# Sums of squares in a gated-delta recurrence: one fp32 product, or two single-pass products of a rounded and a remaining part

## The reference

```python
def gdn_mixer(h, w_in, w_conv, a_log, dt_bias, w_onorm, w_out):
    proj = h @ w_in
    ...
    qkv = jax.nn.silu(causal_conv(qkv, w_conv))
    q, k, v = jnp.split(qkv, 3, axis=-1)
    ...
    q = q * lax.rsqrt(jnp.sum(q * q, axis=-1, keepdims=True) + EPS) * (1.0 / math.sqrt(d))
    k = k * lax.rsqrt(jnp.sum(k * k, axis=-1, keepdims=True) + EPS)
    ...
    o = chunk_gated_delta(q, k, v, g, beta)
    o = o * lax.rsqrt(jnp.mean(o * o, axis=-1, keepdims=True) + EPS) * w_onorm.astype(jnp.float32)
    return (o.reshape(B_, S, GDN_WIDTH) * jax.nn.silu(z)) @ w_out
```

## Time and profile before

| | us |
|---|---|
| median of 3 runs | 2057.92 (2056.8 to 2059.51) |
| span of the profiled execution | 2055.0 |
| TensorE busy | 2017.8 (98%) |
| VectorE busy | 1465.0 (71%) |
| ScalarE busy | 569.1 (28%) |
| GpSimd busy | 354.7 (17%) |

### The profile page before, as it was taken

One profiled execution on the slowest core, in us unless ns is written; L12 is line 12 of the kernel. 1 busy time (PEld: TensorE's weight loads), 2 busy tenths in 40 slices (PEclk: granted clock), 3 DMA queues, 4 the chain that ended last, 5 costly groups with the idle time before them and its releaser, 6 DMA issues.

```text
span 2055.0 us, 31779 instructions
## 1 busy us (share of the span) xinstructions
PE 2017.8 (98%) x12910; PEld 1621.5 (79%) x12910; DVE 1465.0 (71%) x2281; ACT 569.1 (28%) x994; POOL 354.7 (17%) x320
## 2 busy tenths in 40 slices
PE   8999999999999999999999999999999999999999
PEld 6888788887777777777778877777888888888887
DVE  5766666667877777667888887566656778949973
ACT  2000122222544444324774234444310010000000
POOL 2212111111101110011111211111112122212221
PEclk9999999999999999999999999999999999999999
DMA  4323222222211121122112332111223332322332
GB/s 161 112 92 103 83 90 86 93 83 75 83 60 57 63 68 61 60 72 82 62 63 73 126 98 88 62 48 45 77 82 103 98 103 92 103 92 93 102 97 88
DMA packets 53361, 173.73 MB, mean 85 GB/s; under 512 B 6336, under 2 KB 6720, under 8 KB 53088
## 3 DMA queue, kind: packets, MB, share of 16 engines
q1 hardware_dynamic: 48112, 161.67, 23.9%
q10 hardware_dynamic: 5104, 10.03, 1.8%
HBM read 169.51 MB, written 2.16 MB: 84 GB/s over the span
## 4 chain that ended last, share of the span: by engine, by line
PE 45%; DVE 6%; ACT 2%; issue 1%; DVEq 0%; ACTq 0%
PE ps_lin L1817 13%; PE ps_lin L1818 13%; PE ps_lin L1819 13%; PE ps_att L1863 4%; PE ps_aux L1863 2%; ACT arena L1271 2%; DVE arena L409 1%; DVE w_lo L409 1%; DVE arena L415 1%; DVE arena L897 1%; PE ps_att L1872 0%; DVE y_lo L409 0%; DVE sq L409 0%; DVE xw_lo L415 0%; DVE x L409 0%
## 5 line engine op out<-in xcount | busy, mean ns | idle before, releaser
L1817 PE MATMUL ps_lin<-xw_hi,w_hi 128*128 128x512 f32 (+1 forms) x1728 | 698.5, 404 | 0.0
L1819 PE MATMUL ps_lin<-xw_hi,w_lo 128*128 128x512 f32 (+1 forms) x1728 | 675.0, 391 | 0.0
L1818 PE MATMUL ps_lin<-xw_lo,w_hi 128*128 128x512 f32 (+1 forms) x1728 | 674.0, 390 | 0.0
L391 POOL TENSOR_SCALAR w_hi<-raw 128x1024 fp32r<-128x1024 f32 (+5 forms) x312 | 349.9, 1122 | 1685.1 <-PE ps_lin L1819 1560.5
L409 DVE TENSOR_TENSOR w_lo<-raw,w_hi 128x1024 fp32r<-128x1024 f32 (+2 forms) x344 | 382.3, 1114 | 48.0 <-POOL w_hi L391 17.6
L1271 ACT ACTIVATE arena<-arena 128x512 f32<-128x512 f32 (+7 forms) x331 | 206.4, 631 | 734.3 <-DVE arena L409 357.6
L1819 PEld LDWEIGHTS ps_lin<-xw_hi,w_lo 128*128 128x128 f32 (+1 forms) x1728 | 322.7, 187 | 71.8
L1817 PEld LDWEIGHTS ps_lin<-xw_hi,w_hi 128*128 128x128 f32 (+1 forms) x1728 | 323.1, 187 | 68.4 <-issue 3.7
L1818 PEld LDWEIGHTS ps_lin<-xw_lo,w_hi 128*128 128x128 f32 (+1 forms) x1728 | 323.4, 187 | 61.1
L409 DVE TENSOR_TENSOR arena<-ps_lin,rstd 128x512 f32<-128x512 f32 (+2 forms) x213 | 146.6, 688 | 201.2 <-PE ps_lin L1819 186.7
L1817 PE MATMUL ps_lin<-y_hi,w_hi 128*128 128x512 f32 (+1 forms) x544 | 205.4, 378 | 1.3 <-DVE w_lo L409 1.1
(11 more groups left out here) (175 smaller groups left out, 1697.2 us busy)
## 6 DMA issues: line engine op xcount, KB each, us to landing
raw<-in_w_up SPq DMA_DIRECT2D x44, 512.0 KB, 3.3
raw<-in_conv_w_in SPq DMA_DIRECT2D x32, 512.0 KB, 3.3
raw<-in_fox_w_in SPq DMA_DIRECT2D x32, 512.0 KB, 3.3
raw<-in_gdn_w_in SPq DMA_DIRECT2D x32, 512.0 KB, 3.2
raw<-in_w_gate SPq DMA_DIRECT2D x24, 512.0 KB, 3.2
raw<-in_swa_w_in SPq DMA_DIRECT2D x20, 512.0 KB, 3.2
raw<-in_w_ml SPq DMA_DIRECT2D x16, 512.0 KB, 3.3
raw<-in_w_down SPq DMA_DIRECT2D x16, 512.0 KB, 3.6
```

Source lines behind the costliest of these rows:

```text
L391: pool.tensor_scalar(w_whole(n, kc * c)[0], w_raw(n, kc * c), 1.0, 0.0, mult, add).then_inc(s("w_rounded"), 1)
L1817: pe.matmul(o, wh, hi, start=first and k == 0, stop=False)
L1818: pe.matmul(o, wh, lo, start=False, stop=False)
L1819: ins = pe.matmul(o, wl, hi, start=False, stop=last and k == kc - 1)
```

## The change

Each square is computed twice on ScalarE: once in fp32 as before, and once rounded to fp32r, into a free part of `y8_hi` (`sq_hi`, two pieces of 256 columns). GpSimd subtracts the rounded from the full square (`sq_lo`), and signals `gdn_sq_low` or `gdn_osq_low`. TensorE multiplies both parts, in fp32r, with fp32r copies of the ones and mean matrices, which VectorE makes at the head of the layer. GpSimd's subtraction is tied to a weight unit: it is issued right behind the rounding of the third unit after the tile (the q or k tile, or the next head's z tile; for the last head behind the unit of the fourth output tile). There is one `sq_hi` and one `sq_lo`, so ScalarE's Squares get waits for the sums that read them. The semaphores of five input DMAs are merged into one.

```diff
--- before.py
+++ after.py
@@ -294,6 +294,10 @@
         A = carve()
         A(2 * XA_H * MEM)
         sq2 = A(3, T)
+        sq_lo = sb("sq_lo", [P, T], f32r)
+        ones_r, mean_r = sb("ones_r", [P, P], f32r), sb("mean_r", [P, P], f32r)
+        sq_hi = y8_hi[:, 1:3, NT * HD:]
+        sq_parts = lambda ap: ap.rearrange("p (a b) -> p a b", a=2)
         rstd_final, mix_w = sb("rstd_final", [P, T]), sb("mix_w", [P, ND])
         swa["sin"] = rstd_final[:]
 
@@ -334,6 +338,11 @@
             src = raw[:, n % RAW, 0:cols]
             return src.rearrange("p (a c) -> p a c", a=2) if n in ASIDE else src
 
+        GDN_LOW = {}
+        for _h in range(GDN_H):
+            GDN_LOW.update({LAST_UNIT[tile_of("gdn_w_in", part * GDN_H + _h)] + SPLIT: ("gdn_sq", 2 * _h + part + 1, 1) for part in range(2)})
+            GDN_LOW[LAST_UNIT[tile_of("gdn_w_in", 3 * GDN_H + _h + 1)] + SPLIT if _h < GDN_H - 1 else LAST_UNIT[tile_of("gdn_w_out", 3)]] = ("gdn_osq", _h + 1, 0)
+
         GDN_FILL = {"tok": 4, "squares": 4, "A": 0, "U0": 3}
         LEVEL_FILL = (0, 2, 2, 1, 1, 2, 1)
         LAST_FILL = sum(GDN_FILL.values())
@@ -361,11 +370,11 @@
                 sp.dma_start(x[:, m, :], a["x"][m]).then_inc(s(X_IN[m][0]), 16)
                 if m in (1, 3):
                     weights((m + 1) // 2)
-            sp.dma_start(mats[:].rearrange("p a b -> p (a b)"), a["mats"]).then_inc(s("mats_in"), 16)
+            sp.dma_start(mats[:].rearrange("p a b -> p (a b)"), a["mats"]).then_inc(s("small_in"), 16)
             sp.dma_start(rows[:], a["rows"]).then_inc(s("small_in"), 16)
             sp.dma_start(freq[:], a["freq"]).then_inc(s("small_in"), 16)
             sp.dma_start(sinks[:], a["sinks"]).then_inc(s("small_in"), 16)
-            sp.dma_start(angle["pos"].bitcast(i32), a["positions"]).then_inc(s("pos_in"), 16)
+            sp.dma_start(angle["pos"].bitcast(i32), a["positions"]).then_inc(s("small_in"), 16)
             for n in range(RAW, len(UNITS)):
                 sp.wait_ge(s("w_split"), n - RAW + 1)
                 weights(n)
@@ -389,6 +398,10 @@
                 elif n >= SPLIT:
                     pool.wait_ge(s("unit_done"), n - SPLIT + 1)
                 pool.tensor_scalar(w_whole(n, kc * c)[0], w_raw(n, kc * c), 1.0, 0.0, mult, add).then_inc(s("w_rounded"), 1)
+                if n in GDN_LOW:
+                    squared, count, at = GDN_LOW[n]
+                    pool.wait_ge(s(squared), count)
+                    pool.tensor_tensor(sq_parts(sq_lo), sq_parts(sq[:, at, :]), sq_hi.bitcast(f32), sub).then_inc(s(squared + "_low"), 1)
 
 
         @block.vector
@@ -521,8 +534,7 @@
             def swa_angles():
 
                 ang, kk, rr = angle["ang"], angle["kk"], swa["sin"]
-                dve.wait_ge(s("pos_in"), 16)
-                dve.wait_ge(s("small_in"), 48)
+                dve.wait_ge(s("small_in"), 80)
                 step(dve.tensor_copy(ang, angle["pos"].bitcast(i32)))
                 step(ts(ang, ang, freq[:], mult))
                 yield
@@ -613,6 +625,8 @@
 
             F = gdn
             R8 = slice(0, 8)
+            dve.tensor_copy(ones_r[:], mat("ones"))
+            dve.tensor_copy(mean_r[:], mat("mean_h")).then_inc(s("mean_set"), 1)
             step(dve.memset(F["u"][:, 0:3], 0.0))
             step(dve.memset(F["ones"][R8, :], 1.0))
             dve.wait_ge(s("rstd_ready"), 3)
@@ -1387,7 +1401,7 @@
 
             F = gdn
             R8 = slice(0, 8)
-            act.wait_ge(s("small_in"), 48)
+            act.wait_ge(s("small_in"), 80)
             step(activation(F["ea"][R8, :], row("gdn_a_log", 8), ACT.Exp))
             act.wait_ge(s("softplus_in"), 2)
             step(activation(F["r3"][R8, :], F["r2"][R8, :], ACT.Abs))
@@ -1426,7 +1440,10 @@
                     act.wait_ge(s("gdn_silu"), 3 * r + part + 1)
                     if 2 * r + part:
                         act.wait_ge(s("gdn_ss"), 2 * r + part)
-                    activation(sq[:, 1, :], dst, ACT.Square).then_inc(s("gdn_sq"), 1)
+                    if part == 0 and r > 1:
+                        act.wait_ge(s("gdn_oss"), r - 1)
+                    activation(sq[:, 1, :], dst, ACT.Square)
+                    activation(sq_hi, sq_parts(dst), ACT.Square).then_inc(s("gdn_sq"), 1)
 
             for part in range(2):
                 for _ in gdn_tile(0, part):
@@ -1502,7 +1519,9 @@
                 if h < GDN_H - 1:
                     use(ACT.Exp)
                 act.wait_ge(s("gdn_out"), h + 1)
-                activation(sq[:, 0, :], ps_att[:, 0, :], ACT.Square).then_inc(s("gdn_osq"), 1)
+                act.wait_ge(s("gdn_ss"), 2 * min(h + 2, GDN_H))
+                activation(sq[:, 0, :], ps_att[:, 0, :], ACT.Square)
+                activation(sq_hi, sq_parts(ps_att[:, 0, :]), ACT.Square).then_inc(s("gdn_osq"), 1)
 
             def gdn_rms(h):
 
@@ -1905,7 +1924,7 @@
             at[:] = (BANKS, 0)
             tile(4 * ND - BANKS)
             tile(ND)
-            pe.wait_ge(s("mats_in"), 16)
+            pe.wait_ge(s("small_in"), 80)
             tile()
             sum_squares(1)
             tile()
@@ -1978,9 +1997,10 @@
 
             def gdn_tile(r, part):
                 if part in (1, 2):
-                    pe.wait_ge(s("gdn_sq"), 2 * r + part)
+                    pe.wait_ge(s("gdn_sq_low"), 2 * r + part)
                     pe.wait_ge(*aux("gdn_rn", 2 * r + part))
-                    mm_last(ps_aux[:], mat("ones"), sq[:, 1, :]).then_inc(s("gdn_ss"), 1)
+                    mm(sq_parts(ps_aux[:]), ones_r[:], sq_hi, True, False)
+                    mm(ps_aux[:], ones_r[:], sq_lo[:], False, True).then_inc(s("gdn_ss"), 1)
 
             def four(o, l, r, start=True, stop=True):
 
@@ -2083,9 +2103,11 @@
             def gdn_squares(h):
 
                 pe.wait_ge(*aux("gdn_rno", h + 1))
-                pe.wait_ge(s("gdn_osq"), h + 1)
-                mm_last(ps_aux[:], mat("mean_h"), sq[:, 0, :]).then_inc(s("gdn_oss"), 1)
-
+                pe.wait_ge(s("gdn_osq_low"), h + 1)
+                mm(sq_parts(ps_aux[:]), mean_r[:], sq_hi, True, False)
+                mm(ps_aux[:], mean_r[:], sq_lo[:], False, True).then_inc(s("gdn_oss"), 1)
+
+            pe.wait_ge(s("mean_set"), 2)
             for r in range(GDN_H + 1):
                 done = [0]
```

## The result

The changed kernel takes 2063.66 us (median of 6 runs, 2062.29 to 2063.91), the kernel before 2056.19 (6 runs, 2054.23 to 2059.51) beside it: a ratio of 1.0035, interval 1.0025 to 1.0045. The forecast was 2056.3 in a range of 2051 to 2063. Total, direction and range were wrong: the products save what was forecast, and a wait for which the forecast had no term takes it back and more.

A forecast was written before the change was run, and what follows sets the result against it. TensorE was taken as the bound, busy 2017.8 of 2055.0 us. Savings of 8.0 against costs of 3.0 (k sites), 2.5 (first round) and 0.9 (last head) gave -1.6: 2057.9 to 2056.3 us, range 2051 to 2063.

The forecast's parts named there:

- What TensorE saves: Per steady round, cheaper products save 0.41 us at k, 0.39 at q, 0.34 at output; 8.0 us in seven rounds.
- GpSimd's subtraction: At each site, GpSimd's new two-input 128x512 operation takes 1.15 us, with ends of 0.62 and 2.1.
- The slower rival: GpSimd's subtraction becomes the bound at the q site, from about 1.5 us on: 2062.7 or 2071 us; chance 0.20.
- output: ... It holds by 1 us: Steady-round output site: subtraction done at 589.7, product at 590.72, so TensorE would not wait; no cost.
- the k bullet's own rule: Two-SBUF-input VectorE instructions and GpSimd instructions reading SBUF exclude each other for the whole instruction; without it, 3.0 us lower.
- The k site: GpSimd gets ahead of VectorE's split, stalling TensorE some 0.5 us in six rounds: 3.0 us, bounds 0 and 6.
- The first round: Subtraction and delayed rounding obstruct VectorE's convolution and scans: 2.5 us at 542.39, bounds 1.0 and 5.
- one more stretch at the lower clock: First round: longer TensorE waits may bring another stretch at the 1.2 GHz level; part of the upper bound of 5 us.
- The last head: Little cover: sum ready 1.2 us later, scaled output 0.8 later; 0.9 us taken, bounds 0.3 and 3.
- The range's upper end, 2063: The 1.6 us subtraction case; beyond it mainly the 2.1 us case and a fall of the clock at both ends.

The follow-up runs named there:

- out_fill: Changed kernel, but at the output sites GpSimd writes zeros instead of subtracting, so it reads nothing: 2054.75 us, ratio 0.9996 to the kernel before.
- all_fill: Changed kernel, but at all 24 sites GpSimd writes zeros instead of subtracting, so it reads nothing: 2048.73 us, ratio 0.9969 to the kernel before.
- out_old: Changed kernel with the eight output sums made as before, q and k sums left as changed: 2055.68 us, ratio 1.0001 to the kernel before.
- mix: late_out with the two-part sum only for q of rounds 1 to 7 and outputs of heads 0 to 6: 2051.02 us, ratio 0.9978.
- gate_first: Changed kernel with VectorE's gate product ahead of the three k and v scalings in heads 1 to 6: 2060.16 us, ratio 1.0020.
- late_out: Changed kernel; for heads 0 to 6 the output subtraction waits for VectorE's last two-SBUF-input operation, product four pieces later: 2054.61 us, ratio 0.9995.
- qk_old: Changed kernel with the sixteen q and k sums made as before, output sums left as changed: 2063.28 us, ratio 1.0039 to the kernel before.

## Why the prediction was wrong

- **What TensorE saves**: right. 0.40 and 0.34 measured for k and outputs against 0.41 and 0.34 forecast. For q, 606.04 to 606.60 is 0.56, as forecast, against 0.95.
- **GpSimd's subtraction**: 1.28 us undisturbed against 1.15 forecast, inside the bounds; 1.47 at outputs, 1.75 once at a k site. The estimate from GPSIMD Engine Reference, 3.1, of the Trainium skill was 1.1; the trace has 1.28, and that decides. The slower rival, which needed over 1.5 us, did not come about: TensorE waits for GpSimd in two places only.
- **"output: ... It holds by 1 us"**: this step failed. The sentence measured the slack of the product alone. The product indeed never waited. But the k bullet's own rule, that the two engines shut each other out, was not applied to the output site, where VectorE has the split pair and five more operations with two SBUF inputs in a row. Nor was it asked who waits for VectorE's next outputs: the gate product had 0.5 us of slack. Missing term: 1.04 us a round (out_fill against changed), 7.3 us in seven rounds. With it, -1.6 becomes +5.7; measured is +7.5. In TensorE's timeline the wait is larger: from the projection piece ahead of the head's first matrix to the one behind it the changed kernel takes 1.21 to 1.24 us more than before, out_fill 0.14 more. These 0.14 are not GpSimd's reads: TensorE comes 0.4 us sooner there, which uses the slack up. With 1.21 a round the sum is +6.9.
- **The k site**: right in mechanism, shown by all_fill, and in size: six rounds of 0.5, 3.0 us, were forecast, and by the same reading of TensorE's pieces the rounds 2 to 7 lose 0.19, 0.51, 0.58, 0.63, 0.52 and 0.50, 2.9 in all. In out_old, where nothing waits for the gate product, q and k sites together lose 0.7 a steady round: 43.36 is 0.11 below before's where the two products save 0.8. The k site has 0.6 of it; the other 0.1 is the gap without a releaser described above.
- **The first round**: right in mechanism and about in size, 2.2 us against 2.5 forecast, though the two profiles side by side do not say so. The changed kernel's first round is only 0.84 longer than before's, but the granted clock fell at different places in them: before, over 542 to 546 us; in the changed kernel to 0.50 over 530 to 533, behind the wait below, where it cost little, since out_fill, with the same first round and no fall, is only 0.17 shorter (29.36). Like with like: out_fill against mix (first-round sums as before), both at 1.00 throughout, 29.36 against 27.18, are 2.2; gate_first and late_out against before and qk_old, all with the clock falling in the second half, 30.9 against 28.7, are 2.2 too. all_fill, without GpSimd's reads, also falls late and takes 29.16, so 1.8 of the 2.2 us go with GpSimd's reads and the longer time that a subtraction takes than a fill. The prediction allowed for one more stretch at the lower clock; no first round here had more than one. The changed kernel's first product:

```profile
528.89 0.50 PE L1882 MATMUL ps_aux<-y_hi,ones_r 128*128 128x512 f32 x1 [1.81 <-POOL sq_lo L404]
```

  Where VectorE loses time in its convolution, the changed kernel and the kernel before:

```profile
527.91 1.20 DVE L425 TENSOR_SCALAR arena<-arena,cols 128x512 f32<-128x512 f32 x1
529.15 2.98 DVE L428 SCALAR_TENSOR_TENSOR arena<-arena,cols 128x512 f32<-128x512 f32 x3
```

```profile
527.35 0.66 DVE L412 TENSOR_SCALAR arena<-arena,cols 128x512 f32<-128x512 f32 x1
528.04 2.33 DVE L415 SCALAR_TENSOR_TENSOR arena<-arena,cols 128x512 f32<-128x512 f32 x3
```

  GpSimd subtracts from 527.57 to 528.83 and then rounds.

- **The last head**: the product began 1.23 us late, and rows 12's 892.55 became 898.45:

```profile
892.99 1.27 POOL L404 TENSOR_TENSOR sq_lo<-sq,y_hi 128x512 fp32r<-128x512 f32 x1 [35.49 <-ACT y_hi L1285]
...
894.41 0.47 PE L1882 MATMUL ps_aux<-y_hi,mean_r 128*128 128x512 f32 x1 [1.23 <-POOL sq_lo L404]
```

  The piece that starts at 887.96 before stands at 892.78 after, 4.82 later; the piece at 892.55 is 5.90 later. So the site costs 1.1 us; 0.9 was forecast.
- **The q and k sites alone** would have been forecast at -0.1 us (-5.6 + 3.0 + 2.5), and out_old, which has only them, measures -0.1 against before. So the loss is the output sites' alone.
- **The range's upper end, 2063**: it left out that an obstruction costs the blocked engine's whole queue, not one instruction.

## What to carry to other kernels

Work that goes to an idle engine is not free if it shuts out a busier one, as GpSimd's reads of SBUF did here. Before placing a GpSimd operation that reads SBUF, list what VectorE does in that window, mark each operation with two SBUF inputs (and do not leave out all with one: the TENSOR_SCALAR above took 0.66 us before, 1.20 beside the subtraction, 0.49 in all_fill), and ask for every one of VectorE's next outputs how long the bounding engine can wait for it. Here the same instruction cost 1.04 us a round beside weight splits and next to nothing beside operations that read PSUM and one SBUF tensor (late_out's 43.26 against out_fill's 43.18).

## What was not expected of the hardware

- GpSimd gets its turn between two VectorE operations that run back to back otherwise. The second half of the split has nothing to wait for (with the fill, which keeps every semaphore, it follows at once), yet the subtraction, which starts during the first half, goes ahead of it: the pair goes from 1.52 to 2.61 us, 1.09 us longer, and the subtraction takes 1.47 in place of 1.28. A GpSimd fill (128x512, 0.53 us), which reads nothing, did not lengthen the pair at all. This agrees with the Trainium skill, SBUF — State Buffer, "Who interferes with whom", which lets a write-only GpSimd instruction pass beside two-input VectorE work.
- The same instructions of the first round take 1.6 us more or less, according to whether the granted clock falls in its second half (mix 27.18 at 1.00 throughout and qk_old 28.76, both with the first round's sums as in the kernel before; out_fill 29.36 and gate_first 30.92, both with the changed ones). Where it fell earlier, over 530 to 533 us in the changed kernel, it cost 0.2. So a comparison of two single profiles of this kernel is uncertain by that much.
